# Decay rows issued two heads at a time ahead of each projection block, and the first norm's sums taken token by token from the arriving rows

## The reference, cut to what matters

```python
def rmsnorm(x, w):
    xf = x.astype(F32)
    y = xf * lax.rsqrt(jnp.mean(xf * xf, axis=-1, keepdims=True) + EPS)
    return y.astype(x.dtype) * w.astype(x.dtype)
...
    # per head: a decay matrix over all pairs of tokens of a chunk
    seg = a_t[..., :, None] - a_t[..., None, :]
    lmat = jnp.exp(jnp.where(lower, seg, -jnp.inf))
    cb = jnp.einsum('bcign,bcjgn->bcgij', cc, bc)
    y_diag = jnp.einsum('bcgrij,bcjgrp->bcigrp', cb[:, :, :, None] * lmat, xdt)
```

## Time and profile before

| | |
|---|---|
| time, median of 3 runs | 1720.76 us (1717.68 to 1722.38) |
| the profiled execution's own time | 1715.8 us |
| its span, first to last instruction | 1714.0 us |
| PE busy | 1649.0 us, 96% of the span |
| DVE, ACT, POOL busy | 1256.0, 987.4, 64.9 us |
| mean granted TensorE clock | 0.954 |

### The profile page before, as it was taken

The page is one execution under the profiler, slowest core; times in us unless marked ns, Lnnn a source line. Parts: engine busy times, 40 slices in busy tenths (PEclk is TensorE's granted clock), DMA queues, the critical chain, the costliest instruction groups (busy, mean ns, idle before and its releaser), DMA issues.

```text
span 1714.0 us, 22061 instructions
## 1 busy us (share of the span) xinstructions
PE 1649.0 (96%) x8331; PEld 1368.6 (80%) x8331; DVE 1256.0 (73%) x1200; ACT 987.4 (58%) x903; POOL 64.9 (4%) x78
## 2 busy tenths in 40 slices
PE   7998689999999998999999999999999999999996
PEld 5775369999959958788888888888888888888885
DVE  4346855666356655688888988898988988988883
ACT  2354443443244603576777776676776777777662
POOL 0122000000010320000000000000000000000000
PEclk8997679999988998899999999999999999999997
DMA  7331014557503503799999999999999999999982
GB/s 250 117 98 50 1 49 148 172 175 209 181 25 123 172 16 133 249 369 345 355 371 344 356 370 341 357 368 343 359 368 343 346 371 341 360 369 332 362 313 74
DMA packets 221093, 429.55 MB, mean 251 GB/s; under 512 B 9490, under 2 KB 76440, under 8 KB 220720
## 3 DMA queue, kind: packets, MB, share of 16 engines
q1 hardware_dynamic: 217528, 423.77, 69.8%
q10 hardware_dynamic: 3512, 5.08, 0.8%
HBM read 427.77 MB, written 1.05 MB: 250 GB/s over the span
## 4 chain that ended last, share of the span: by engine, by line
PE 91%; DVE 4%; ACT 2%; DMA 1%; issue 1%; ACTq 0%; DVEq 0%; SPq 0%
PE ps L1504 89%; PE ps L1516 2%; DVE arena L1070 1%; ACT arena L588 1%; DVE ring_lo L1124 0%; DVE arena L963 0%; DMA raw<-in_moe_w_up_dram 0%; DMA arena<-in_meta_tokens_dram 0%; DMA raw<-in_moe_w_gate_dram 0%; DMA raw<-in_moe_w_down_dram 0%; ACT w_hi L857 0%; ACT arena L812 0%; DVE arena L1234 0%; DVE xn L1134 0%; ACT arena L672 0%
## 5 line engine op out<-in xcount | busy, mean ns | idle before, releaser
L1295 DVE TENSOR_TENSOR w_lo<-raw,w_hi 128x2048 fp32r<-128x2048 f32 x224 | 511.9, 2291 | 78.9 <-ACT w_hi L857 77.2
L857 ACT ACTIVATE w_hi<-raw 128x2048 fp32r<-128x2048 f32 x224 | 429.1, 1919 | 177.2 <-DMA raw<-in_moe_w_up_dram 88.1
L1504 PE MATMUL ps<-w_hi,xg_hi 128*128 128x512 f32 x896 | 355.7, 397 | 2.3 <-DVE xg_lo L1391 1.4
L1504 PE MATMUL ps<-w_hi,xg_lo 128*128 128x512 f32 x896 | 350.4, 391 | 0.0
L1504 PE MATMUL ps<-w_lo,xg_hi 128*128 128x512 f32 x896 | 349.9, 391 | 0.0
L1299 DVE TENSOR_TENSOR w_lo<-raw,w_hi 128x2048 fp32r<-128x2048 f32 x112 | 256.2, 2288 | 55.7 <-ACT w_hi L861 55.2
L861 ACT ACTIVATE w_hi<-raw 128x2048 fp32r<-128x2048 f32 x112 | 214.9, 1919 | 93.6 <-DMA raw<-in_moe_w_down_dram 91.9
L1504 PEld LDWEIGHTS ps<-w_hi,xg_lo 128*128 128x128 f32 x896 | 168.9, 188 | 36.3
L1504 PEld LDWEIGHTS ps<-w_hi,xg_hi 128*128 128x128 f32 x896 | 169.0, 189 | 36.0 <-DVE xg_lo L1391 1.6
L1504 PEld LDWEIGHTS ps<-w_lo,xg_hi 128*128 128x128 f32 x896 | 169.2, 189 | 33.4
L1504 PE MATMUL ps<-w_hi,eh_hi 128*128 128x512 f32 x448 | 176.9, 395 | 7.7 <-DVE eh_lo L1384 6.9
(11 more groups left out here) (264 smaller groups left out, 1990.7 us busy)
## 6 DMA issues: line engine op xcount, KB each, us to landing
raw<-in_moe_w_gate_dram SPq DMA_DIRECT2D x112, 1024.0 KB, 5.1
raw<-in_moe_w_up_dram SPq DMA_DIRECT2D x112, 1024.0 KB, 5.1
raw<-in_moe_w_down_dram SPq DMA_DIRECT2D x112, 1024.0 KB, 5.0
ring<-in_w_in_ab_dram SPq DMA_DIRECT2D x12, 1024.0 KB, 5.4
ring<-in_hy_w_in_dram SPq DMA_DIRECT2D x12, 1024.0 KB, 5.1
ring<-in_ffn_w_gate_dram SPq DMA_DIRECT2D x11, 1024.0 KB, 5.4
ring<-in_ffn_w_up_dram SPq DMA_DIRECT2D x11, 1024.0 KB, 5.4
ring<-in_ffn_w_down_dram SPq DMA_DIRECT2D x8, 1408.0 KB, 7.2
```

The costliest lines, as they stand in the source:

```text
L857: nc.scalar.activation(w_hi[:, j, :], raw[:, j, :], ACT.Copy).then_inc(sem("gu_high"), 1)
L1295: V.tensor_tensor(w_lo[:, j, :], raw[:, j, :], w_hi[:, j, :].bitcast(F32), ALU.subtract).then_inc(sem("gu_split"), 1)
L1504: return nc.tensor.matmul(o, l, r, start=start, stop=stop)
```

## The change

There are two parts.

*Start and norm.* SP's queue requests `x` in two halves of 128 tokens, one norm weight row, and weight blocks 0 and 1, ahead of the other 24 parameter rows; it no longer waits for `x` or for the rows, and blocks 2 and 3 follow the rows. ACT requests only the 64 KB identity of the table and the meta tokens before its work; the rest of the table goes with the later request. The square sums are taken by token from the untransposed rows: ACT squares the meta rows and the first half with an accumulated sum, DVE squares the second half and reduces it; one small root and one small reciprocal give a factor per token on its partition; DVE multiplies the identity by it (three diagonal tiles), and three products of ones with the diagonals (`ss1`) spread the factors over all partitions, from where DVE's eight products read them in PSUM. A new tile `nme` turns the norm's weight. The turning of the other parameters (`param`) moves behind projection block 0 on PE, and behind the copy of `proj` 0 on ACT.

*Decay stage.* Four steps, each with the rows of two heads (four tiles), one projection block (6 to 9) and, from the second step on, `y` of the pair before; then block 10, the last `y`, block 11. ACT makes both heads' Relu, then alternates Exp and the copy of a projection tile. The rotary products wait for 20 projection tiles instead of 24. DVE's and POOL's loops over the heads are unchanged.

```diff
-K_FIRST = K_AT["uf"][0]
+K_FIRST = K_AT["perm"][0]
...
     add("xin", 0, 5)
+    add("nme", 0)
+    add("ss1", 0)
+    add("proj", 0, 2)
     add("param", 0)
-    add("ss1", 0)
-    add("proj", 0, 4)
+    add("proj", 2, 2)
...
-    for s in range(10):
-        if s < 8:
-            add("row", 2 * s, 2)
-        if s < 6:
-            add("proj", 12 + 2 * s, 2)
-        if s >= 3 and s % 2 == 1:
-            add("y", (s - 3) // 2)
+    for step in range(4):
+        add("row", 4 * step, 4)
+        add("proj", 12 + 2 * step, 2)
+        if step:
+            add("y", step - 1)
+    add("proj", 20, 2)
+    add("y", 3)
+    add("proj", 22, 2)
...
+            for tt in range(2):
+                sp.dma_start(xtok[:, tt, :], A["x"][0, tt * P:(tt + 1) * P, :]).then_inc(sem(f"x{tt}_in"), 16)
+            sp.dma_start(prow[C_NME:C_NME + KT, 0, :], A["norm_mix_even"].rearrange("e (t p) -> (e t) p", p=P)).then_inc(sem("nme_in"), 16)
+            for n, (src, k) in enumerate(stream[0:2]):
+                sp.dma_start(slot(n, k), src).then_inc(slot_in[n % RING], 16)
...
-            sp.wait_ge(sem("x_in"), 32)
-            sp.wait_ge(sem("param_in"), 16 * 25)
             for n, (src, k) in enumerate(stream):
+                if n < 2:
+                    continue
...
             act.dma_start(ktab[:, 0:K_FIRST], A["k_table"][:, 0:K_FIRST]).then_inc(sem("ident_in"), 16)
-            act.dma_start(xtok, A["x"][0].rearrange("(t p) d -> p t d", p=P)).then_inc(sem("x_in"), 16)
-            act.dma_start(mtok[0:META, :], A["meta_tokens"]).then_inc(sem("x_in"), 16)
+            act.dma_start(mtok[0:META, :], A["meta_tokens"]).then_inc(sem("meta_in"), 16)
...
+            act.wait_ge(sem("pool_consts"), 4)
             sqrt_table()
-            root("ss1", 0, D)
+            act.wait_ge(sem("meta_in"), 16)
+            a(nc.scalar.activation(row_squares[0:META, :], mtok[0:META, :], ACT.Square, accum_out=xsum[0:META, 2:3]))
+            act.wait_ge(sem("x0_in"), 16)
+            a(nc.scalar.activation(row_squares, xtok[:, 0, :], ACT.Square, accum_out=xsum[:, 0:1]))
+            turned_in(0)
+            turned_in(1)
+            act.wait_ge(sem("x1_sum"), 1)
+            a(nc.scalar.activation(xsum[:, 0:3], xsum[:, 0:3], ACT.Sqrt, bias=eps[:, 0:1], scale=1.0 / D), sem("x_root"))
+            turned_in(2)
+            turned_in(3)
+            turned_in(4)
...
-            for s in range(9):
-                if s < 8:
-                    if s >= 4:
-                        act.wait_ge(sem("tile_ready"), NUMBER[("y", (s - 4) // 2)] + 1)
-                    decay_rows(s)
...
+            for step in range(4):
+                for h in (2 * step, 2 * step + 1):
+                    if step >= 2:
+                        act.wait_ge(sem("tile_ready"), NUMBER[("y", step - 2)] + 1)
+                    decay_rows(h)
+                for k in range(2):
+                    decay_exp(2 * step + k)
+                    projected(12 + 2 * step + k)
+            for j in range(20, 24):
+                projected(j)
...
+            dve.wait_ge(sem("x1_in"), 16)
+            v(V.tensor_tensor(row_squares, xtok[:, 1, :], xtok[:, 1, :], ALU.mult))
+            v(V.tensor_reduce(xsum[:, 1:2], row_squares, AX.X, ALU.add), sem("x1_sum"))
+            t = ready(dve, "nme", 0)
+            v(V.tensor_copy(par[:, C_NME:C_NME + KT], t[:, 0:KT]), used("nme"))
+            dve.wait_ge(sem("x_root"), 1)
+            v(V.reciprocal(xsum[:, 0:3], xsum[:, 0:3]))
+
+            for tt, (t0, n) in enumerate(((META, P), (META + P, P), (0, META))):
+                v(V.tensor_scalar(rstd[0:n, t0:t0 + n], ident[0:n, 0:n], xsum[0:n, tt:tt + 1], None, ALU.mult), sem("rstd_diag"))
             dve.wait_ge(used("xin"), 5)
-            square(4, 8, sem("dve_squares"))
+            t = ready(dve, "ss1", 0)
+            for k in range(KT):
+                mult_add(xn[:, k, :], t[:, 0:T], par[:, C_NME + k:C_NME + k + 1], hT[:, k, :], sem("xn1_ready"), ALU.mult, ALU.mult)
+            V.memset(crd[:, 7:8], 0.0).then_inc(used("ss1"), 1)
             dve.wait_ge(used("param"), 1)
-            norm("ss1", C_NME, s=sem("xn1_ready"))
...
+            for tt, (t0, n) in enumerate(((META, P), (META + P, P), (0, META))):
+                pe.wait_ge(sem("rstd_diag"), tt + 1)
+                last = mm(o[:, t0:t0 + n], ones[0:n, :], rstd[0:n, t0:t0 + n])
+            close(last)
+
+            def parameters():
+                pe.wait_ge(sem("param_in"), 16 * 24)
...
+            for step in range(4):
+                for h in (2 * step, 2 * step + 1):
+                    for way in range(2):
+                        o = open_tile("row", 2 * h + way)
+                        close(mm(o[:, 0:T], sel8[:, P * h:P * h + P], csr[0:HEADS, way, :]))
+                linear("proj", 12 + 2 * step, 6 + step, xn)
+                if step:
+                    state_output(step - 1)
+            linear("proj", 20, 10, xn)
+            state_output(3)
+            linear("proj", 22, 11, xn)
+            pe.wait_ge(used("proj"), 20)
```

More of the change, by code:

```diff
@@ L357, in trunk @@
         mtok = area(13952, D)
+        xsum = area(17344, 4)
         pr = area(11904, 2, 2, T)
@@ L600, in square, with turned_in @@
                 a(nc.scalar.activation(sq[:, lo:hi, toks], hT[:, lo:hi, toks], ACT.Square), sem("act_squares"))
-            for tt in range(2):
-                for half in range(2):
-                    t = ready(act, "xin", 2 * tt + half)
+            def turned_in(k):
+                t = ready(act, "xin", k)
+                if k < 4:
+                    tt, half = k // 2, k % 2
                     a(nc.scalar.activation(hT[:, 4 * half:4 * half + 4, META + P * tt:META + P * tt + P],
                                            t[:, :].rearrange("p (a b) -> p a b", a=4), ACT.Copy), used("xin"))
-            t = ready(act, "xin", 4)
@@ L609, in _ @@
[L609 to L615, removed]
@@ L646, in _ @@
                 copy("proj", j, xp[:, j, 2:2 + T])
+                if j == 0:
+                    parameters()
                 if j >= 1:
@@ L679, in decay_exp, with projected @@
                 a(nc.scalar.activation(M[0:META, h % 4, 2, :], M[0:META, h % 4, 2, :], ACT.Exp, scale=-1.0), sem("decay_ready"))
-            for s in range(9):
-                if s < 8:
-                    if s >= 4:
-                        act.wait_ge(sem("tile_ready"), NUMBER[("y", (s - 4) // 2)] + 1)
-                    decay_rows(s)
[L686 to L695, removed]
+            def projected(j):
+                if j < 16:
+                    copy("proj", j, qk[:, j - 12, :], scale=64.0 ** -0.5)
+                elif j < 20:
+                    copy("proj", j, qk[:, j - 12, :])
+                else:
+                    copy("proj", j, vf[:, j - 20, :])
+            for step in range(4):
[8 more added lines that the diff above has]
+                projected(j)
             act.wait_ge(sem("yz_ready"), 4)
@@ L1610, in _, with state_output @@
             pe.wait_ge(used("xs"), 3)
-            for s in range(10):
-                if s < 8:
-                    for way in range(2):
-                        o = open_tile("row", 2 * s + way)
-                        close(mm(o[:, 0:T], sel8[:, P * s:P * s + P], csr[0:HEADS, way, :]))
-                if s < 6:
-                    linear("proj", 12 + 2 * s, 6 + s, xn)
-                if s >= 3 and s % 2 == 1:
-                    pair = (s - 3) // 2
-                    o = open_tile("y", pair)
-                    for h in (2 * pair, 2 * pair + 1):
-                        pe.wait_ge(sem("m_ready"), h + 1)
-                        r = 64 * (h % 2)
-                        for tt, (t0, n) in enumerate(TOKS):
-                            last = mm(o[r:r + 64, 0:T], xT[0:n, tt, 64 * h:64 * h + 64], M[0:n, h % 4, tt, :], tt == 0, tt == 2)
-                    close(last)
-            pe.wait_ge(used("proj"), 24)
+            def state_output(pair):
+                o = open_tile("y", pair)
+                for h in (2 * pair, 2 * pair + 1):
+                    pe.wait_ge(sem("m_ready"), h + 1)
+                    r = 64 * (h % 2)
+                    for tt, (t0, n) in enumerate(TOKS):
+                        last = mm(o[r:r + 64, 0:T], xT[0:n, tt, 64 * h:64 * h + 64], M[0:n, h % 4, tt, :], tt == 0, tt == 2)
+                close(last)
+            for step in range(4):
+                for h in (2 * step, 2 * step + 1):
+                    for way in range(2):
+                        o = open_tile("row", 2 * h + way)
[7 more added lines that the diff above has]
+            pe.wait_ge(used("proj"), 20)
             for j in range(8):
```

43 lines of the change are left out of this document (28 added, 15 removed).

## The result

| | before | changed |
|---|---|---|
| median, 4 runs each on the same chip | 1719.22 us (1716.03 to 1722.38) | 1698.86 us (1696.34 to 1700.55) |
| profiled execution's span | 1714.0 us | 1697.5 us |
| mean granted clock | 0.954 | 0.956 |

The account below looks back on a forecast made before the run. PE holds 91% of the path, so time comes off only where it waits, runs at half clock or loses work. Start 10.1 plus decay stage 7.6 gives 17.7 us saved, a median of 1703 us, 8-in-10 range 1696 to 1711.

Parts of the forecast that it names:

- The start: Up to the projection: first product at 12.0 us instead of 22.65; 10.1 us saved net, bounds 7 and 13.3.
- `nme` hold the reciprocal: In the start: DVE's copy of the turned norm weight, by 9.7 us, holds the reciprocal; ACT's root is ready at 8.9.
- costed at nothing: In the start: ACT's own squares finish before x's second half is summed, so cost nothing; without that cover 1.3 us.
- SP issues them by about 10.5, 9 us to spare: Parameter rows on SP's queue: issued by about 10.5 us, landing near 13, asked for by PE at about 22.
- The clock at the start: First two projection blocks: the same 2.6 us half-clock loss as before, with +2.6 and -1.5 as ends.
- The decay stage: First decay row to first rotary product: 73.2 us instead of 78.6, saving 5.4, bounds 10.9 and 2.3.
- The PSUM wait of the fourth step: Decay stage: the fourth step's first row tile waits 1.6 us for y 0's bank, which DVE reads late.
- don't add: Decay stage: clock falls up to 6 us and PSUM waits of 2.6 overlap, so 5.5 us together.
- Behind the stage: First rotary product to the maximum chain: 10.8 us instead of 13.0, saving 2.2, bounds 0.8 and 2.3.
- (1): Rival: the decay stage gives nothing net and only the start counts, 1710.7 or 1708 us; chance 20%.
- (3): Rival: transfers collide with the 3.4 MB table, PE waits for blocks 2 and 3; 1706 to 1709 us; chance 5%.
- (4): Rival: slower, PE's clock stays at half through steps 1 to 3 and blocks 10 and 11; 1741 us; chance 3%.
- (2): Rival: both parts gain in full, no dip and full clock at the start; 25 us saved, 1696; chance 12%.

Follow-up runs that it names:

- s3: The changed kernel run and traced again with no edit: 1700.76 us, ratio 0.9909 to the kernel before.
- t3: The changed kernel with weight blocks 0 and 1 requested behind the parameter rows again: first projection product waits for block 0, at 15.73 us.
- t1: The changed kernel with DVE's read of a finished y moved into its wait for ACT's Exp: decay stage 71.44 us.
- s2: The kernel before with only the new decay loops, start as before: 1711.37 us, ratio 0.9968; decay stage 72.58 us.
- s1: The changed kernel with the decay loops of before, so only start and norm are new: 1705.01 us, ratio 0.9943.
- v1: u2 with the rotary products between the last y and block 11, k by cos on DVE instead of GpSimd: 1690.81 us, ratio 0.9854.
- v2: v1 with ACT's Exp of lambda and its squares of the mixer's output moved forward: 1686.78 us, ratio 0.9846.
- t6: The changed kernel with y between a block's two tiles and DVE's read of y before the decay sum of heads 4 and 6: stage 67.46 us.
- u2: The changed kernel with t6's edits, t5's edit, ACT squaring x's first half first and the norm weight copied behind the diagonals: 1693.80 us, ratio 0.9862.
- t2: The changed kernel with y of the pair before put between the two tiles of each projection block: decay stage 76.30 us.
- t5: The changed kernel with the 24 parameter rows requested between weight blocks 0 and 1: first row's request 0.51 us instead of 3.64.

## Why the prediction was right, point by point

**The sum.** Forecast 1703 with 17.7 us saved; measured 1698.9, with 16.5 us in the spans and 14 to 22 by the interval. Of the 4.2 us between forecast and median, 1.5 are the baseline's (its median over four runs is 1719.22, not 1720.76); 2.7 are left, no step explains them, and the four runs of one kernel spread by 4 to 6 us. That 16.5 is near 17.7 is in part luck: term by term the traces differ from the forecast by +0.5 (up to the dt products), -1.4 (from there to the first row), +0.6 (decay stage), -1.4 (behind it) and +0.5 (the rest), and these cancel.

**The start: size right in one trace, holder open.** First product at 12.7, forecast 12.0; 13.6 in s3. The second half of x came at 6.9, not 6.1. The first 64 KB on ACT's queue took 4.6 us from issue to landing, more than the 3.3 of 400 KB in the earlier trace rows; what delays either is open, and t3 speaks against the weights queued behind. The reduction took 1.22 us (forecast 1.3), the diagonals 0.87 (0.9), the root 0.30 (0.2). I had `nme` hold the reciprocal and ACT's root ready before it. In the first trace it was ACT, by 0.1 us: its list began with the meta rows at 6.2, and the root started 0.5 us behind DVE's sum. ACT's squares, costed at nothing, cost that. In s3 the copy of `nme` came last, as forecast, since PE turned more slowly there. The two are within 0.3 us of each other, and how fast PE turns decides which it is (4.32 us in the first trace, 4.63 in s3).

**The parameter turning.** 0.49 us on the path, as forecast (0.54). The step "SP issues them by about 10.5, 9 us to spare" failed: SP's request of the first row stood 3.6 us behind two 1 MB blocks, and the last went out at 14.3. In one trace (t1) it went out at 14.75 and PE waited for it until 23.65. In the others PE did not wait; by how much the rows came earlier is not shown.

**The clock at the start.** Taken as unchanged. The first two blocks took 16.8 us without the turning in between, against 17.7 before; but s2, with the start of before, took 15.4, and the changed start gives 16.7 to 17.8, so the 0.7 us of that station lies within the scatter. From the dt products to the first row the changed kernel lost 1.4 us, a term that the sum didn't have. It isn't the change: this stretch takes 48.3 to 48.6 us in four of the fourteen traces and 49.7 to 50.0 in ten, among the four are three with the new start, and s2 has 49.95. The profiled execution of before was one of the four.

**The decay stage: size right, mechanism half.** 72.6 against 73.2. The layout of the heads was right within 0.5 us: pairs ended 16.4, 29.7, 44.1 and 58.2 us behind the first row, forecast 16.3, 29.5, 43.6 and 57.7, and `m_ready` was never waited for. PE's work was put too high, at 67.7: it is 66.5, as four rows take 2.02 us and not 2.22, and y 3.32 and not 3.39. The PSUM wait of the fourth step was there, 1.0 us (forecast 1.6), the one before block 10 was not. I said that falls of the clock and PSUM waits "don't add" and then took 5.5 us for both as a guess. They were 6.0: in the first trace 1.7 (fall) + 1.0 (wait) + 3.3 (fall), in s3 2.7 (wait) + 3.3 (fall). So two errors of 1.2 and 0.5 us partly cancelled. s3 shows the rule behind the 6.0: up to the bank of y 0, the pace is DVE's and ACT's pair of heads, 13.4 us a pair (forecast 13.2), so a fall ahead of the wait costs nothing, and only the one behind it (3.3 us over rows and block in both traces) counts.

**Behind the stage.** Forecast 2.2 saved, measured 0.8, the lower bound. The full clock for the rotary products was right (3.83), but the step that gave its gain to DVE's rotary work failed. Two arms lead to the maximum: DVE's rotary work with PE's first scores, and ACT's squares, roots, copies and lambda with PE's sums of squares. In the kernel before ACT's held, and DVE stood for it:

```profile
180.07 0.16 DVE L1064 TENSOR_TENSOR lam<-lam 128x1 f32<-128x1 f32 x1 [2.11 <-ACT lam L707]
```

The sums of squares stand behind the rotary products on PE, so the full clock shortened ACT's arm: lambda's Exp ended 12.9 us behind the first rotary product before and 10.8 after. DVE's arm did not shorten. It started 0.7 us earlier, but took 10.6 us instead of 9.5: three of its products took 0.67 to 0.88 us instead of 0.44, all three beside POOL's four products (152.68 to 156.24), which in the kernel before had run before the stretch began. So DVE's arm, 0.5 us longer than ACT's, became the holder:

```profile
153.08 0.67 DVE L1092 TENSOR_TENSOR arena<-arena,ktab 128x272 f32<-128x272 f32 x1
153.78 0.88 DVE L1097 TENSOR_TENSOR arena<-arena 128x272 f32<-128x272 f32 x1
...
162.51 0.20 ACT L736 ACTIVATE lam<-lam 128x2 f32<-128x2 f32 x1
162.74 0.44 DVE L1097 TENSOR_TENSOR arena<-arena,xn 128x272 f32<-128x272 f32 x1
```

In s1, v1 and v2, where POOL does nothing in this stretch, all of DVE's rotary products take 0.44 us. That the two engines slow each other is likely, but no run has changed that alone.

**The rivals.** (1) fell: the stage gave 6.0 us, alone too (s2). (3) fell as priced, block 2 held no one in any trace; what was short was the parameter rows. (4) never showed: the clock came back within each block. (2) did not come: the fourth step fell to half clock in every trace of this order; a stage without a fall came only with other edits (67.4 to 67.5 us in t6 and u2). The rule of the Trainium skill (TensorE: Matmul & The Clock Gate, HAM oscillation — how this bites in real kernels), that it is idling which makes the clock fall, does not cover the fall at 105 here, with PE busy at 1.00 before it, just as at 129 before.

## What to carry to other kernels

Reordering PE's list also reorders the banks: for every moved tile ask which tile had its bank and when the reading engine, in its own order, gets to it. A read moved ahead of work that waits for another engine anyway cost nothing (head 4 ends at the same time in t2 and t6), and it turned a new order that lost 3.7 us (t2) into one that gained 5.1 (t6). Before costing a stage by PE's clock, find out whether PE sets its pace; and where an arm of a path is shortened, measure the arm beside it before counting the gain.

## What the runs showed that I had not expected

- A request of a 20 KB row took 3.3 to 3.6 us on SP's queue right behind two blocks of 1 MB (seven traces), 0.51 behind one (t5, u2, v1, v2), and 0.29 behind none (t3). A small transfer's place in the request order is worth microseconds of issue time alone.
- The same program had the clock fall at different blocks in different executions (at 103.77 in the first trace, not in s3's 105.67), behind the same thin products. With y and the rows apart and the read early (t6, u2) no block of the stage fell.
- 64 KB landed 4.6 us after its request, 400 KB in the kernel before 3.3 us after its own, both as the first request of ACT's queue at 0.72. The difference is not explained.
